# Layer norms taken by halves of 272 tokens, their variance by four groups of 32 PSUM rows, and the retention heads unrolled

## The chip, the core and the metric

The kernel runs on one core of a Trainium2 chip. The metric is the device time of one execution in microseconds; three executions of the kernel before gave 1895.0, 1896.52 and 1900.74 us, median 1896.52 us. The profiled execution is one of its own, with its own time.

## The reference, cut to what matters

Two decoder layers over 512 prompt tokens and 32 sample tokens, 544 in all, of width 1024. Layer 0 mixes by a chunk gMLP and stick-breaking attention, layer 1 by a retention with four heads. Each mixer and each feed-forward part ends in a residual addition and a layer norm over the 1024 features, so there are four layer norms:

```python
def _layer_norm(x, g, b):
    mu = jnp.mean(xf, axis=-1, keepdims=True)
    var = jnp.mean(jnp.square(xf - mu), axis=-1, keepdims=True)
    y = (xf - mu) * lax.rsqrt(var + LN_EPS)
    return y * g + b
# layer 0:  x <- LN(ALPHA*x + W_out_ab [gMLP | attention])     norm 0
# layer 1:  x <- LN(ALPHA*x + W_out_ret (silu(g) * HeadNorm(Retention)))   norm 2
# every l:  x <- LN(ALPHA*x + W_down(gelu(conv3(x W_gate)) * x W_val))     norms 1 and 3
```

The outputs are y for all tokens, new keys, values and states, and the convolution states.

## The kernel before, in words

Activations lie with features on the 128 partitions and the 544 tokens along the row: y[:, m, :] is feature block m of 8 (KD = 8). A product of weights and activations goes by output tiles of 128 features. Each weight tile is loaded by a DMA into w_raw, split by ScalarE (w_hi) and VectorE (w_lo, the function low), and multiplied in three terms (w_hi x_hi, w_hi x_lo, w_lo x_hi) for each block kt of 128 input features; x_hi and x_lo are the same split of the activations. Tokens go in two halves of 272 columns (HN), each half into a PSUM bank of its own, so a tile takes k times 3 times 2 matmuls, k being 8 after a norm or the attention, 11 (KF) in the down product and 4 in the retention's output product. All of them stand in part_body (L1267). Tiles alternate between two slots j = 0, 1: banks 0 and 1 for j = 0, banks 2 and 3 for j = 1, and one w_raw, w_hi and w_lo buffer for each j. A weight tile u can be split once tile u - 2 is done (tile_done), and TensorE starts tile u when w_lo is there (lo_ready) and its banks are free (evicted[j]).

The order on each engine is written out by hand, in program order, with semaphores between engines; nothing is scheduled. Around a norm it is this. VectorE adds each finished output tile to y and to the running sum s1 (add_up, L986 and L990). After the last tile TensorE sums s1 over the partitions (the mean, L1527, banks 4 and 5), VectorE subtracts it from the 8 blocks (L1009), ScalarE squares them (L589) into two slots of sq, and TensorE adds the squares of each block up over the partitions (L1532, banks 6 and 7). ScalarE takes Ln and Exp (L592, L594), VectorE sharpens the result by one Newton step (L1019, L1021, L1024) and scales the blocks (L1013), ScalarE shifts them into x_hi (L599; into y at the end, L602), and VectorE makes x_lo (L1034). TensorE's next product waits for x_lo block by block (ln_done). Meanwhile GpSimd prepares the residual for the next addition (L417) once all 8 blocks of x_lo stand, and the first two weight tiles of the next product have been split before the norm begins. The third one is split when the first tile of the next product is done.

After norm 1 VectorE also waits for GpSimd's scaling of y and for a zeroed tile before it goes on. The four retention heads are one loop on every engine. At the end y is stored by 8 DMAs, one for each block.

## Time and profile before

| what | us |
|---|---|
| median of three executions | 1896.52 |
| profiled execution, its own time | 1897.47 |
| its span | 1895.7 |
| TensorE busy in the span | 1778.9 |
| VectorE busy | 893.0 |
| ScalarE busy | 529.2 |
| mean granted clock of TensorE | 0.974 |

The time of the profiled execution is 1.8 us longer than its span and 1.0 us above the median. Matmuls overlap, so a busy time of TensorE close to the span says only that it seldom stood still. A row of a timeline gives the start, the time to the end of its last instruction, the engine and line, what is written and read, the count, and in brackets how long the engine had been idle and what it had waited for. A granted clock of 1.00 is TensorE's level of 2.4 GHz, 0.50 that of 1.2 GHz.

### The profile page before, as it was taken

To read this page: it belongs to the slowest core of one execution; us is meant where nothing else is said; L and a number is where in the kernel's file an instruction comes from. 1 tells how busy PE (TensorE), PEld (TensorE's weight loads), DVE (VectorE), ACT (ScalarE), POOL (GpSimd) and SP (SyncE) were. 2 spreads that over 40 slices of the span, in tenths; PEclk is the share of its full clock that TensorE was granted. 3 is DMA by queue.
4 is the path that set the end of the run, shared out by engine and by line. 5 is a ranking of instruction groups with operands and counts; after the bars stand their busy time and mean duration, and the time that the engine had idled before them with its cause. 6 is when DMAs were issued, how large, how long until landed. Compare 5 with 4: busy or idle time off the path is not lost.

```text
span 1895.7 us, 35052 instructions
## 1 busy us (share of the span) xinstructions
PE 1778.9 (94%) x13474; PEld 1591.3 (84%) x13474; DVE 893.0 (47%) x1435; ACT 529.2 (28%) x742; POOL 151.3 (8%) x137
## 2 busy tenths in 40 slices
PE   8998996979999999979989989989987999999996
PEld 8765674869999999969679759849947999999995
DVE  3444355566542555352362263263256655245543
ACT  3324233242221222142222222222223322122213
POOL 0000002001000000014003013013010100000000
PEclk9999998899999999999989999999998999999998
DMA  8889784112222223212242333333323223222221
GB/s 285 297 297 302 234 306 161 45 45 89 88 99 79 78 89 105 80 38 94 104 156 97 118 133 100 129 127 105 140 89 100 71 89 106 82 78 89 89 93 47
DMA packets 84221, 234.65 MB, mean 124 GB/s; under 512 B 9777, under 2 KB 10066, under 8 KB 83778
## 3 DMA queue, kind: packets, MB, share of 16 engines
q1 hardware_dynamic: 80834, 218.97, 34.0%
q0 software_dynamic: 3328, 14.92, 2.2%
q8 instruction: 34, 0.56, 0.1%
q14 instruction: 25, 0.20, 0.0%
HBM read 210.05 MB, written 23.80 MB: 123 GB/s over the span
## 4 chain that ended last, share of the span: by engine, by line
PE 66%; issue 25%; DVE 5%; ACT 2%; POOL 1%; DMA 1%; SPq 0%; DVEq 0%; ACTq 0%; POOLq 0%
PE banks L1267 50%; PE banks L1612 2%; PE banks L1619 2%; PE banks L1604 1%; PE banks L1532 1%; PE banks L1294 1%; PE banks L1369 1%; PE banks L1382 1%; PE banks L1592 1%; PE banks L1330 1%; POOL y L417 1%; PE banks L1358 1%; PE banks L1635 1%; DVE x_lo L1034 1%; PE banks L1372 1%
## 5 line engine op out<-in xcount | busy, mean ns | idle before, releaser
L1267 PE MATMUL banks<-x_hi,w_hi 128*128 128x272 f32 x2624 | 551.7, 292 | 33.4 <-DVE x_lo L1034 22.3
L1267 PE MATMUL banks<-x_hi,w_lo 128*128 128x272 f32 x2624 | 545.8, 290 | 0.0
L1267 PE MATMUL banks<-x_lo,w_hi 128*128 128x272 f32 x2624 | 544.9, 289 | 0.0
L694 DVE TENSOR_TENSOR w_lo<-w_raw,w_hi 128x1024 fp32r<-128x1024 f32 (+2 forms) x228 | 284.9, 1250 | 514.6 <-ACT w_hi L462 514.5
L462 ACT ACTIVATE w_hi<-w_raw 128x1024 fp32r<-128x1024 f32 (+2 forms) x228 | 238.2, 1045 | 942.3 <-PE banks L1267 913.2
L1267 PEld LDWEIGHTS banks<-x_hi,w_hi 128*128 128x128 f32 x2624 | 415.0, 190 | 51.8 <-issue 32.5
L1267 PEld LDWEIGHTS banks<-x_lo,w_hi 128*128 128x128 f32 x2624 | 416.0, 190 | 0.0
L1267 PEld LDWEIGHTS banks<-x_hi,w_lo 128*128 128x128 f32 x2624 | 413.6, 190 | 0.0
L1267 PE MATMUL banks<-act_lo,w_hi 128*128 128x272 f32 x704 | 145.3, 287 | 0.0
L1267 PE MATMUL banks<-act_hi,w_hi 128*128 128x272 f32 x704 | 145.1, 287 | 0.0
L1267 PE MATMUL banks<-act_hi,w_lo 128*128 128x272 f32 x704 | 145.1, 287 | 0.0
L986 DVE TENSOR_TENSOR y<-y,banks 128x544 f32 (+1 forms) x40 | 28.9, 721 | 188.6 <-PE banks L1267 188.6
L1267 PEld LDWEIGHTS banks<-act_hi,w_lo 128*128 128x128 f32 x704 | 110.3, 188 | 0.0
L1267 PEld LDWEIGHTS banks<-act_lo,w_hi 128*128 128x128 f32 x704 | 110.3, 188 | 0.0
L1267 PEld LDWEIGHTS banks<-act_hi,w_hi 128*128 128x128 f32 x704 | 110.2, 188 | 0.0
L1267 PE MATMUL banks<-m_hi,w_hi 128*128 128x272 f32 x256 | 57.7, 309 | 8.7 <-DVE m_lo L1197 8.7
L436 POOL TENSOR_TENSOR onat<-rqk,rope 128x544 f32<-128x544 f32 x32 | 46.6, 1486 | 154.4 <-ACT rqk L643 154.4
L1267 PE MATMUL banks<-m_lo,w_hi 128*128 128x272 f32 x256 | 56.2, 303 | 0.0
L1267 PE MATMUL banks<-m_hi,w_lo 128*128 128x272 f32 x256 | 56.1, 302 | 0.0
L449 POOL TENSOR_SCALAR km<-kp,cst 96x256 fp32r<-96x256 f32 x32 | 29.7, 932 | 302.5 <-DVE kp L1119 173.9
L1267 PEld LDWEIGHTS banks<-m_hi,w_hi 128*128 128x128 f32 x256 | 44.0, 206 | 9.2 <-issue 9.2
L1144 DVE SCALAR_TENSOR_TENSOR s<-s,tab,banks 128x1024 f32<-128x1024 f32 x32 | 40.5, 1277 | 16.0 <-PE banks L1635 15.9
(232 smaller groups left out, 1714.3 us busy)
## 6 DMA issues: line engine op xcount, KB each, us to landing
w_raw<-in_w_up SPq DMA_DIRECT2D x88, 512.0 KB, 3.2
kv<-in_kc SPq DMA_DIRECT2D x128, 256.0 KB, 4.8
kv<-in_vc SPq DMA_DIRECT2D x128, 256.0 KB, 4.4
w_raw<-in_w_rin SPq DMA_DIRECT2D x48, 512.0 KB, 3.3
w_raw<-in_w_dn SPq DMA_DIRECT2D x32, 704.0 KB, 4.1
s<-in_s SPq DMA_DIRECT2D x32, 512.0 KB, 7.3
out_ret_s<-s SPq DMA_DIRECT2D x32, 512.0 KB, 2.6
w_raw<-in_w_in_ab POOLq DMA_DIRECT2D x16, 512.0 KB, 6.1
```

Of the source, the lines that this page charges most:

```text
L417: nc.gpsimd.tensor_scalar(y[:, m, :], y[:, m, :], lnp[:, n, 1, m:m + 1], ALPHA, ALU.add, ALU.mult)\
L436: step.add(nc.gpsimd.tensor_tensor(t[n], a, rope[:, c, :], ALU.mult))
L449: nc.gpsimd.tensor_scalar(km[:, b % 2, :], kp[:, :].bitcast(F32), blockm[:, b:b + 1], None, ALU.mult).then_inc(km_ready, 1)
L462: return nc.scalar.activation(out, in_, ACT.Copy)
L694: V.tensor_tensor(w_lo[:, j, 0:k * P], w_raw[:, j, 0:k * P], w_hi[:, j, 0:k * P].bitcast(F32), ALU.subtract).then_inc(lo_ready, 1)
L986: V.tensor_tensor(out, out, bank_pair(j), ALU.add).then_inc(evicted[j], 1)
L1034: V.scalar_tensor_tensor(x_lo[:, m, :], y[:, m, :], lnp[:, n, 1, m:m + 1], x_hi[:, m, :].bitcast(F32), ALU.add, ALU.subtract)\
L1144: V.scalar_tensor_tensor(old, old, tab[:, T_CD:T_CD + 1], banks, ALU.mult, ALU.add)\
L1267: last = mm(B[:, 2 * j + half, 0:HN], a[:, j, w], x[:, kt, half * HN:(half + 1) * HN], start=kt == 0 and n == 0, stop=kt == k - 1 and n == 2)
L1294: last = mm(B[32 * r:32 * r + 32, 4, k * P:(k + 1) * P], qz[:, c, :], kv[:, s, g, c * P:(c + 1) * P], start=c == 0, stop=c == 3)
L1612: last = mm(B[:, bank, :], scT[:, c0:c0 + P], rvn[:, j, :], start=j == 0, stop=j == t)
L1619: last = mm(B[rows, 3, :], qm[:, dt, b, :], s0[:, b % RING, dt, :], start=False, stop=b >= DEC_B - 4 and dt == 1)
```

## The change

A norm is taken for tokens 0 to 271 (half 0) and 272 to 543 (half 1) apart, and its work is put between the products before and behind it.

- TensorE: the last two tiles of the product before a norm (last_pair) run half 0 of both tiles first and half 1 of both after it. Between the steps of half 1, at places that a table names, stand half 0's mean, the two parts of its variance and the sum of its parts (spread). The first two tiles of the product behind the norm (first_pair) run half 0 first, with half 1's mean, variance and spread between its steps, and then half 1. The mean takes two matmuls (s1 and y's block 7) in place of one.
- The variance: four squares lie in sq at a time, and each is multiplied into 32 rows of its own of the PSUM bank. ScalarE copies the bank to s1, divided by 32, and a matmul with ones adds the rows up.
- VectorE: half 0 and half 1 in a written order. The evictions of the last two tiles, and the w_lo splits of the next product's first two tiles, stand inside the norm. ScalarE likewise, with the w_hi splits.
- The norms' instructions on VectorE and ScalarE held 128 x 544 elements; each is now two of 128 x 272.
- The heads are unrolled on all engines. VectorE's wait for the zeroed tile stands after the first head's products, and its wait for GpSimd's scaling of y ahead of the output addition.
- GpSimd waits for x_lo of both halves. y is stored by 16 DMAs, half 0 first.

The diff, cut; the removed lines of norm on each engine stand in the kernel above.

```diff
...
+PLACES = {KF: ((0, 3), (0, 10), (1, 4), (1, 7)), KD: ((0, 3), (1, 1), (1, 6), (1, 7)), 4: ((0, 3), (1, 3), (1, 3), (1, 3))}
...
+        def sq_slot(m):
+            return sq[:, m % 4 // 2, cols(m % 2)]
...
+            for half in range(2):
+                for m in range(KD):
+                    sp.wait_ge(y_final, half * KD + m + 1)
+                    sp.dma_start(A["yT"][:, m, cols(half)], y[:, m, cols(half)]).then_inc(y_stored, 16)
...
+            def norm(n, u):
                 nc.scalar.preload_act_table_set("natural_log_exp_and_others")
...
+                def squares(half, first, end):
+                    for m in range(first, end):
+                        q = half * KD + m
+                        act.wait_ge(c_ready, 2 * n * KD + q + 1)
+                        if q >= 4:
+                            act.wait_ge(sq_used, 4 * n + q // 4)
+                        nc.scalar.activation(sq_slot(m), y[:, m, cols(half)], ACT.Square).then_inc(sq_ready, 1)
+                def parts(half):
+                    act.wait_ge(sq_used, 4 * n + 2 * half + 2)
+                    nc.scalar.activation(s1[:, cols(half)], B[:, 6 + half, 0:HN], ACT.Copy, scale=1.0 / 32)\
+                        .then_inc(part_ready, 1)
+                def deviation(half):
+                    act.wait_ge(var_done, 2 * n + half + 1)
+                    step.add(nc.scalar.activation(std[:, cols(half)], B[:, 6 + half, 0:HN], ACT.Ln, bias=eps))
+                    step.wait()
+                    nc.scalar.activation(std[:, cols(half)], std[:, cols(half)], ACT.Exp, scale=-0.5)\
+                        .then_inc(std_ready, 1)
+                def shift(half, first, end):
+                    for m in range(first, end):
+                        act.wait_ge(scaled, (2 * n + half) * KD + m + 1)
+                        dst, done = (x_hi, lnhi_ready) if n < 3 else (y, y_final)
+                        nc.scalar.activation(dst[:, m, cols(half)], y[:, m, cols(half)], ACT.Identity,
+                                             bias=lnp[:, n, 1, m:m + 1]).then_inc(done, 1)
+                squares(0, 0, 4)
+                if u is not None:
+                    split(u, 0, KD)
+                squares(0, 4, KD)
+                parts(0)
+                deviation(0)
+                shift(0, 0, 3)
+                if u is not None:
+                    split(u + 1, 1, KD)
+                for m in range(3, KD):
+                    shift(0, m, m + 1)
+                    squares(1, 2 * m - 6, min(2 * m - 4, KD))
+                parts(1)
+                deviation(1)
+                shift(1, 0, KD)
...
+            def norm(n, base, u):
+                def take(half, j):
+                    i = N_OUT - 2 + j
+                    if half == 0:
+                        dve.wait_ge(half_done, 2 * n + j + 1)
+                    else:
+                        dve.wait_ge(tile_done, base + i + 1)
+                    last = V.tensor_tensor(y[:, i, cols(half)], y[:, i, cols(half)], B[:, 2 * j + half, 0:HN], ALU.add)
+                    if half:
+                        last.then_inc(evicted[j], 1)
+                    elif j:
+                        last.then_inc(s_sum, 1)
+                    else:
+                        step.add(last)
+                    if j == 0:
+                        if half:
+                            dve.wait_ge(evicted[0], (base + N_OUT) // 2 + 1)
+                        else:
+                            step.wait()
+                        step.add(V.tensor_tensor(s1[:, cols(half)], s1[:, cols(half)], y[:, i, cols(half)], ALU.add))
+                def centre(half):
+                    dve.wait_ge(m_done, 2 * n + half + 1)
+                    for m in range(KD):
+                        V.tensor_tensor(y[:, m, cols(half)], y[:, m, cols(half)], B[:, 4 + half, 0:HN], ALU.subtract)\
+                            .then_inc(c_ready, 1)
+                def inverse(half):
+                    own, first, var = s1[:, cols(half)], std[:, cols(half)], B[:, 6 + half, 0:HN]
+                    dve.wait_ge(std_ready, 2 * n + half + 1)
+                    step.add(V.tensor_tensor(own, first, first, ALU.mult))
+                    step.wait()
+                    step.add(V.scalar_tensor_tensor(own, var, eps, own, ALU.add, ALU.mult))
+                    step.wait()
+                    step.add(V.scalar_tensor_tensor(first, own, 3.0, first, ALU.subtract, ALU.mult))
+                    step.wait()
+                    dve.wait_ge(c_ready, (2 * n + half + 1) * KD)
+                def scale(half, m):
+                    V.scalar_tensor_tensor(y[:, m, cols(half)], y[:, m, cols(half)], lnp[:, n, 0, m:m + 1],
+                                           std[:, cols(half)], ALU.mult, ALU.mult).then_inc(scaled, 1)
+                def rest(half, m):
+                    if n < 3:
+                        dve.wait_ge(scaled, (2 * n + half) * KD + m + 1)
+                        dve.wait_ge(lnhi_ready, (2 * n + half) * KD + m + 1)
+                        V.scalar_tensor_tensor(x_lo[:, m, cols(half)], y[:, m, cols(half)], lnp[:, n, 1, m:m + 1],
+                                               x_hi[:, m, cols(half)].bitcast(F32), ALU.add, ALU.subtract)\
+                            .then_inc(ln_done[half], 1)
+                def tail(half, first):
+                    for m in range(first, KD):
+                        scale(half, m)
+                        rest(half, m - 1)
+                    rest(half, KD - 1)
                 step.wait()
...
+                take(0, 0)
                 step.wait()
...
+                take(0, 1)
+                dve.wait_ge(s_sum, 2 * n + 1)
+                centre(0)
+                take(1, 0)
                 step.wait()
...
+                if u is not None:
+                    low(u, 0, KD)
+                inverse(0)
+                scale(0, 0)
+                scale(0, 1)
+                take(1, 1)
+                dve.wait_ge(evicted[1], (base + N_OUT) // 2 + 1)
+                dve.sem_inc(s_sum, 1)
+                rest(0, 0)
+                scale(0, 2)
+                rest(0, 1)
+                scale(0, 3)
+                rest(0, 2)
+                centre(1)
+                scale(0, 4)
+                rest(0, 3)
+                if u is not None:
+                    low(u + 1, 1, KD)
+                scale(0, 5)
+                rest(0, 4)
+                tail(0, 6)
+                inverse(1)
+                scale(1, 0)
+                tail(1, 1)
...
-            dve.wait_ge(y_scaled, 1 + 2 * KD)
-            dve.wait_ge(zeroed, 3)
...
+                dve.wait_ge(zeroed, 3)
...
+                dve.wait_ge(y_scaled, 1 + 2 * KD)
...
+            def half_step(j, half, k, hi, lo, kt):
+                w = slice(kt * P, (kt + 1) * P)
+                for n, (a, x) in enumerate(((w_hi, hi), (w_hi, lo), (w_lo, hi))):
+                    last = mm(B[:, 2 * j + half, 0:HN], a[:, j, w], x[:, kt, cols(half)],
+                              start=kt == 0 and n == 0, stop=kt == k - 1 and n == 2)
+                return last
+            def mean(n, half):
+                if half:
+                    pe.wait_ge(s_sum, 2 * n + 2)
+                else:
+                    pe.wait_ge(s_sum, 2 * n + 1)
+                mm(B[:, 4 + half, 0:HN], mean_mat, s1[:, cols(half)], start=True, stop=False)
+                mm(B[:, 4 + half, 0:HN], mean_mat, y[:, KD - 1, cols(half)], start=False, stop=True).then_inc(m_done, 1)
+            def variance(n, half, m0):
+                pe.wait_ge(sq_ready, (2 * n + half) * KD + m0 + 4)
+                for g in range(4):
+                    last = mm(B[32 * g:32 * g + 32, 6 + half, 0:HN], mean_mat[:, 0:32], sq_slot(m0 + g),
+                              start=m0 == 0, stop=m0 == 4)
+                last.then_inc(sq_used, 1)
+            def spread(n, half):
+                pe.wait_ge(part_ready, 2 * n + half + 1)
+                mm(B[:, 6 + half, 0:HN], ones, s1[:, cols(half)], start=True, stop=True).then_inc(var_done, 1)
+            def last_pair(n, base, k, hi, lo):
+                for half in range(2):
+                    for j in range(2):
+                        u = base + N_OUT - 2 + j
+                        if half == 0:
+                            pe.wait_ge(lo_ready, u + 1)
+                            pe.wait_ge(evicted[j], u // 2 + 1)
+                        for kt in range(k):
+                            last = half_step(j, half, k, hi, lo, kt)
+                            if half:
+                                for at, what in zip(PLACES[k], ((mean, ()), (variance, (0,)), (variance, (4,)), (spread, ()))):
+                                    if at == (j, kt):
+                                        what[0](n, 0, *what[1])
+                        last.then_inc(half_done if half == 0 else tile_done, 1)
+            def first_pair(n, base):
+                def step_of(half, j, kt):
+                    if j == 0:
+                        pe.wait_ge(ln_done[half], n * KD + kt + 1)
+                    elif kt == 0:
+                        pe.wait_ge(lo_ready, base + 2)
+                        pe.wait_ge(evicted[1], base // 2 + 1)
+                    last = half_step(j, half, KD, x_hi, x_lo, kt)
+                    if half and kt == KD - 1:
+                        last.then_inc(tile_done, 1)
+                pe.wait_ge(lo_ready, base + 1)
+                pe.wait_ge(evicted[0], base // 2 + 1)
+                step_of(0, 0, 0)
+                mean(n, 1)
+                step_of(0, 0, 1)
+                step_of(0, 0, 2)
+                variance(n, 1, 0)
+                step_of(0, 0, 3)
+                step_of(0, 0, 4)
+                variance(n, 1, 4)
+                step_of(0, 1, 0)
+                step_of(0, 1, 1)
+                step_of(0, 0, 5)
+                spread(n, 1)
+                for kt in range(2, 6):
+                    step_of(0, 1, kt)
+                for kt in range(6, KD):
+                    step_of(0, 0, kt)
+                for kt in range(6, KD):
+                    step_of(0, 1, kt)
+                for kt in range(KD):
+                    step_of(1, 0, kt)
+                    if kt >= 2:
+                        step_of(1, 1, kt - 2)
+                for kt in range(KD - 2, KD):
+                    step_of(1, 1, kt)
...
-            product(U_OUT_AB, N_OUT, KD, x_hi, x_lo, mixed)
-            norm(0)
+            product(U_OUT_AB, N_OUT - 2, KD, x_hi, x_lo, mixed)
+            last_pair(0, U_OUT_AB, KD, x_hi, x_lo)
             ffn(0)
-            norm(1)
-            with pe.Fori(0, H_C) as h:
-                with pe.Fori(0, N_RIN // 2) as i:
+            last_pair(1, U_RET - N_OUT, KF, act_hi, act_lo)
...
```

In the rows below, s is s1, cst holds the constant matrices (the mean's and ones) and banks is PSUM. The first place is VectorE from the last tile of the product before norm 0 on. Before:

```order
L986 TENSOR_TENSOR y<-y,banks 128x544
L990 TENSOR_TENSOR s<-s,y 128x544
L694 TENSOR_TENSOR w_lo<-w_raw,w_hi 128x1024
L1009 TENSOR_TENSOR y<-y,banks 128x544 x8
L1019 TENSOR_TENSOR s<-std 128x544
L1021 SCALAR_TENSOR_TENSOR s<-banks,cst,s 128x544
L1024 SCALAR_TENSOR_TENSOR std<-s,std 128x544
L1013 SCALAR_TENSOR_TENSOR y<-y,lnp,std 128x544 x2
L1034 SCALAR_TENSOR_TENSOR x_lo<-y,lnp,x_hi 128x544
```

And the changed kernel on VectorE, from half 0's mean (L1070) to half 1's (the second L1070):

```order
L1070 TENSOR_TENSOR y<-y,banks 128x272 x8
L1053 TENSOR_TENSOR y<-y,banks 128x272
L1065 TENSOR_TENSOR s<-s,y 128x272
L735 TENSOR_TENSOR w_lo<-w_raw,w_hi 128x1024
L1076 TENSOR_TENSOR s<-std 128x272
L1078 SCALAR_TENSOR_TENSOR s<-banks,cst,s 128x272
L1080 SCALAR_TENSOR_TENSOR std<-s,std 128x272
L1085 SCALAR_TENSOR_TENSOR y<-y,lnp,std 128x272 x2
L1053 TENSOR_TENSOR y<-y,banks 128x272
L1092 SCALAR_TENSOR_TENSOR x_lo<-y,lnp,x_hi 128x272
...
L1070 TENSOR_TENSOR y<-y,banks 128x272 x8
```

The eviction of the last tile's half 1 (the second L1053) now stands ahead of the first x_lo, and half 1's subtraction follows after three blocks of half 0's x_lo.

The second place is TensorE between the product before norm 0 and the one behind it. Before, the norm stands between the two:

```order
L1267 MATMUL banks<-x_hi,w_lo 128x272 x2
L1250 REGISTER_ALU
L1250 COMPARE_AND_BRANCH
L1527 MATMUL banks<-s,cst 128x272 x2
L1532 MATMUL banks<-sq,cst 128x272 x16
L1250 UNCONDITIONAL_BRANCH
```

In the changed kernel, from the last step of last_pair to half 1's first variance (L1376 is the spread, L1364 and L1365 the mean, L1370 the variance):

```order
L1376 MATMUL banks<-s,cst 128x272
L1355 MATMUL banks<-x_hi,w_hi 128x272
L1355 MATMUL banks<-x_lo,w_hi 128x272
L1355 MATMUL banks<-x_hi,w_lo 128x272
L1364 MATMUL banks<-s,cst 128x272
L1365 MATMUL banks<-y,cst 128x272
...
L1355 MATMUL banks<-x_hi,w_lo 128x272
L1370 MATMUL banks<-sq,cst 32x272 x4
```

One step of the next product stands between half 0's spread and half 1's mean, and two more before the variance; the sixteen wide matmuls of the variance are now four times four narrow ones.

## Rows read from the trace of the kernel before

**Rows 1.** Timeline of TensorE at norm 0: start us, us, engine and line.
```profile
396.44 0.41 PE L1267 MATMUL banks<-x_hi,w_lo 128*128 128x272 f32 x2
398.49 1.18 PE L1527 MATMUL banks<-s,cst 128*128 128x272 f32 x4 [1.64 <-DVE s L990]
401.17 6.08 PE L1532 MATMUL banks<-sq,cst 128*128 128x272 f32 x24 [1.50 <-ACT sq L589]
...
415.94 0.79 PE L1267 MATMUL banks<-x_hi,w_hi 128*128 128x272 f32 x2 [6.42 <-DVE x_lo L1034]
...
425.17 0.52 PE L1267 MATMUL banks<-x_hi,w_hi 128*128 128x272 f32 x2
```
**Rows 2.** Windows: us, busy PE, PEld, DVE, ACT, POOL, granted clock, DMA share, GB/s.
```profile
426.00:808.00 382.00, 382.00 (x3056) 382.00 (x3055) 188.92 (x321) 92.92 (x146) 6.47 (x7) 1.00 0.26 88
```
**Rows 3.** Timeline of VectorE at norm 0.
```profile
399.71 5.14 DVE L1009 TENSOR_TENSOR y<-y,banks 128x544 f32<-128x544 f32 x8
411.00 0.73 DVE L1019 TENSOR_TENSOR s<-std 128x544 f32<-128x544 f32 x1 [6.15 <-ACT std L594]
...
415.01 0.79 DVE L1034 SCALAR_TENSOR_TENSOR x_lo<-y,lnp,x_hi 128x544 fp32r<-128x544 f32 x1 [0.19 <-ACT x_hi L599]
415.71 0.78 DVE L1013 SCALAR_TENSOR_TENSOR y<-y,lnp,std 128x544 f32<-128x544 f32 x1
...
427.32 1.79 DVE L694 TENSOR_TENSOR w_lo<-w_raw,w_hi 128x1024 fp32r<-128x1024 f32 x1 [2.19 <-ACT w_hi L462]
```
**Rows 4.** Timeline of ScalarE at norm 0.
```profile
400.46 1.29 ACT L589 ACTIVATE sq<-y 128x544 f32<-128x544 f32 x2 [1.16 <-DVE y L1009]
...
426.23 1.06 ACT L462 ACTIVATE w_hi<-w_raw 128x1024 fp32r<-128x1024 f32 x1 [0.70 <-PE banks L1267]
```
**Rows 5.** Timeline of VectorE in layer 0's feed-forward part.
```profile
434.52 0.43 DVE L1066 TENSOR_TENSOR af<-ge,banks 128x272 f32<-128x272 f32 x1
434.87 0.40 DVE L1067 TENSOR_TENSOR af<-ge,banks 128x240 f32<-128x240 f32 x1
```
**Rows 6.** Groups of ScalarE's instructions: count, busy us, mean ns, idle before.
```profile
L462 ACT ACTIVATE gp<-banks 128x272 f32<-128x272 f32 x132 | 32.1, 316 | 0.0
L599 ACT ACTIVATE x_hi<-y,lnp 128x544 fp32r<-128x544 f32 x24 | 17.8, 749 | 22.0 <-DVE y L1013 22.0
```
**Rows 7.** Timeline of TensorE in the attention, four products of 32 rows each.
```profile
241.27 1.10 PE L1330 MATMUL banks<-kv,ad 128*32 128x512 f32 x8 [0.35 <-DMA kv<-in_vc]
```
**Rows 8.** Windows of TensorE alone at norms 0 and 3: us, busy, clock.
```profile
413.00:420.00 7.00, 4.06 (x18) 0.51 0.00 0
1870.60:1877.40 6.80, 5.30 (x13) 0.50 0.00 0
```
**Rows 9.** Timeline of TensorE at norm 1.
```profile
816.12 0.41 PE L1267 MATMUL banks<-act_hi,w_lo 128*128 128x272 f32 x2
...
853.33 0.49 PE L1267 MATMUL banks<-x_hi,w_hi 128*128 128x272 f32 x2 [1.71 <-DVE w_lo L694]
```
**Rows 10.** Timeline of VectorE behind norm 1.
```profile
851.64 0.07 DVE L1097 MEMSET rmv<- 128x10 f32 x1 [7.12 <-POOL qm L426]
```
**Rows 11.** Timeline of TensorE at norm 2.
```profile
1447.54 0.41 PE L1267 MATMUL banks<-m_hi,w_lo 128*128 128x272 f32 x2
...
1466.82 0.79 PE L1267 MATMUL banks<-x_hi,w_hi 128*128 128x272 f32 x2 [6.42 <-DVE x_lo L1034]
```
**Rows 12.** Timeline of VectorE ahead of norm 2's last tile.
```profile
1443.40 0.69 DVE L694 TENSOR_TENSOR w_lo<-w_raw,w_hi 128x512 fp32r<-128x512 f32 x1
```
**Rows 13.** Timelines of TensorE and ScalarE at norm 3.
```profile
1867.29 0.41 PE L1267 MATMUL banks<-act_hi,w_lo 128*128 128x272 f32 x2
...
1872.54 10.31 PE L1532 MATMUL banks<-sq,cst 128*128 128x272 f32 x32 [1.50 <-ACT sq L589]
...
1887.49 5.62 ACT L602 ACTIVATE y<-y,lnp 128x544 f32<-128x544 f32 x8 [3.19 <-DVE y L1013]
```
**Rows 14.** The chain that ended last, across the end of a head (start us, us).
```profile
966.88 99.39 PE banks L1267 x768
```

More of the change, by code:

```diff
@@ L339, in _ @@
             load_ffn(0)
-            with sp.Fori(0, H_C) as h:
+            for h in range(H_C):
                 base = h * N_RET + U_RET
@@ L427, in _ @@
             pool.wait_ge(rope_in, 16)
-            with pool.Fori(0, H_C) as h, step.loop(h, H_C, 8):
+            for h in range(H_C):
                 for qk in range(2):
@@ L1678, in _ @@
                         tile_body(j, 4, m_hi, m_lo)
-            norm(2)
+            last_pair(2, U_FFN[1] - N_OUT, 4, m_hi, m_lo)
             ffn(1)
-            norm(3)
-RET_STEPS = 14 + 9
+            last_pair(3, U_ALL - N_OUT, KF, act_hi, act_lo)
+            mean(3, 1)
+            for m in (0, 4):
+                variance(3, 1, m)
+            spread(3, 1)
 def decays(h):
```

174 lines of the change are left out of this document (64 added, 110 removed).

## The prediction

> **What bounds the kernel now.** I read the windows over the products first. In layer 0's feed-forward part TensorE is busy for 382 of 382 us at the full clock, with 3056 matmuls, one each 0.125 us [rows 2]. There nothing can be won but by fewer matmuls, and the change leaves their number. Then I read TensorE's timeline at the norms. The last matmul of the product before norm 0 starts at 396.44, the next product's first at 415.94, and its last step only at 425.17 [rows 1]: 48 matmuls that need 6.0 us take 10. So I take as one stretch the time from the start of the last pair of tiles to the start of the third tile behind the norm; everything that the change moves lies in it.
>
> Before, the stretches are these, with 0.125 us for a matmul. Norm 0: the pair has 96 matmuls, so it starts at 396.69 - 12.0 = 384.7; the third tile starts at 425.17 + 0.75 + 6.0 = 431.9; 47.2 us. Norm 1: 132 matmuls, 816.37 - 16.5 = 799.9, to 853.33 [rows 9]; 53.5. Norm 2: 48 matmuls, 1447.8 - 6.0 = 1441.8; its product starts at 1466.82 [rows 11] and runs as norm 0's, 16.0 more to 1482.8; 41.0. Norm 3: 1867.54 - 16.5 = 1851.0, to the last shift's end at 1893.1 [rows 13]; 42.1, with the last store behind it in both kernels.
>
> VectorE's and ScalarE's timelines show what fills a gap: subtraction (5.14), squares behind it, Ln and Exp, three Newton operations, then scaling and x_lo in turn, 1.4 us a block [rows 3, 4]. TensorE waits 6.42 us for the first x_lo and after it goes at VectorE's pace [rows 1, 3].
>
> **The costs of a half.** A 272-column operation of VectorE that takes two tensors lasts 0.43 and lets the next start after 0.35 [rows 5]; I take 0.36. The scaling kind lasts 0.79 at 544 columns and starts every 0.70 [rows 3]; 272 columns less are 0.28 less, so 0.50 and 0.41. Two dependent ones cost the first's whole duration. ScalarE: a square 1.29 / 2 less 0.28, so 0.36, Ln and Exp 0.4 each, copy 0.32, shift 0.75 less 0.28, so 0.47 [rows 4, 6]. A fp32 mean matmul is 1.18 / 2, less the tail, so 0.50 [rows 1]. A handover between engines is 0.05 to 0.2 with the matmul's own tail.
>
> Four 32-row products: in the attention four of 512 columns took 1.10 us together [rows 7], so they ran side by side: one of 512 columns alone takes about 0.5 x 512 / 272 = 0.94. For 272 columns that is 0.6. The variance falls from 16 x 0.5 = 8.1 us (6.08 for three quarters [rows 1]) to 4 x 0.6. Added are two mean matmuls and two spreads, 2.0, and two copies of 0.3. TensorE's own work in a norm goes from 9.3 to about 5.4.
>
> **Norm 0, step by step**, from the pair's start. Half 0 of both tiles ends at 6.0. VectorE adds the last tile by 6.8. The mean stands four steps (0.375 each) into half 1, 7.6 to 8.6. VectorE subtracts 8.75 to 11.6, the eighth square ends at 13.0 (a weight split of 1.0 lies between), the second variance part 13.3 to 13.9, the copy, the spread to 14.9. That hides this half's norm behind half 1's matmuls but for its end: Ln and Exp to 16.0, three Newton operations to 17.6, two scalings, the last eviction, x_lo to 19.4. TensorE starts at 19.5, idle 4.5. Half 1's mean ends at 20.9. VectorE, after three blocks of x_lo, subtracts from 21.0 to 23.9, then scales block 4. Only behind that may ScalarE shift block 4 and make squares 3 and 4 (25.6): TensorE, which stands in order at the variance, waits 4.0. The next one waits for squares 7 and 8: 28.7, another 1.5. Spread to 30.9, Ln, Exp, Newton, two scalings and x_lo to 35.2; TensorE has had ten steps of half 0 to do meanwhile and idles 1.3. Then VectorE gives a block every 0.83 and TensorE two steps in 0.75, to 41.0, and three steps are left: 42.4.
>
> Then a wait that was not there. The third tile's weights can be split once tile 1 is done. Before, the second tile (6.0 us) covered that. Now the two tiles end 1.1 apart. The split takes 1.06 [rows 4]; w_lo takes 1.79 beside GpSimd's residual work, which again starts at this moment [rows 3]. With handovers that is 3.2 less 1.1: 2.1 of idle TensorE. Queued behind w_lo on VectorE is the first convolution, for which nothing waits for 6 us. Norm 0: 44.5 against 47.2, -2.7 at the full clock.
>
> **The other norms**, by the same steps. Norm 1's pair is longer by 36 matmuls, so the first half's chain ends under it but for x_lo, which now waits for the last eviction: idle 3.4. I get 45.8 + 2.1 = 47.9 against 53.5: -5.6. In it is the old wait of 1.71 for w_lo, caused by VectorE's wait for the zeroed tile [rows 9, 10]; that goes, and the 2.1 come in its place. Norm 2's pair has 48 matmuls, half 1 of it 3.0 us, which cover little: its last tile starts after 1.5 but its w_lo is there after 2.3 [rows 12], 0.8 lost, the variance parts wait 0.7 and 1.8, the spread 0.6. 40.0 + 2.1 against 41.0: +1.1. Norm 3: half 1's mean at 22.2, variance 28.0 and 30.6, shifts end 38.8 against 42.1: -3.3. The sum at the full clock is -10.5.
>
> **The clock.** Before, TensorE's clock was 0.51 from 413 to 420, after the 6.4 us of idleness, and 0.50 from 1870.6 to 1877.4 [rows 8], where it had only waited twice for 1.5 to 2 us with a mean between. So the level of 1.2 GHz comes after sparse stretches, not only after empty ones, and lasts some 7 us. Before, it cost little in norms 0 to 2, since x_lo set the pace. Now half 1's mean, variance and spread stand in the chain. With 1.2 GHz from 19 to 31 or so, the mean costs 1.0 more, the steps in front of it 0.3, variance and spread 0.5 each: 2.3 in norm 0, 1.7 in norm 1, 2.3 in norm 2 (its spread and two variances), 1.4 in norm 3. The ends are 0 and 3.2 each, the latter with the clock low from 16 to 34. Taken: 2.3 + 1.7 + 2.3 + 1.4 = 7.7. The norms then stand at -0.4, -3.9, +3.4 and -1.9: -2.8.
>
> The Trainium skill, "TensorE: Matmul & The Clock Gate", section "HAM oscillation — how this bites in real kernels", tells of a loop whose waits throttle the clock again at every turn. By it the bursts and waits of each first pair would pay more than once; that is the second rival below. No row here shows such a pattern at a norm.
>
> **Heads unrolled.** The chain runs from 966.88 for 99.39 us through 768 matmuls and over a head's end [rows 14]; at 0.125 these need 96.0 and the rest is slow ones at the stretch's start, so the loop's turn costs TensorE nothing. What may go is register work ahead of waits; what may come is longer code to fetch. Neither has a row. I bound it by -3 and +4 for all heads and take -1. VectorE's later wait for y's scaling, 16 DMAs for 8 at the end, and the GpSimd waits: nothing, each is ready long before; the last store starts with the last shift as before.
>
> **The sum.** -2.8 - 1 = -3.8. The profiled execution took 1897.47, 1.0 above the median; against the median of 1896.5 I predict 1892.7.
>
> **The rivals.** First, the chains are tighter or the clock stays up: the times between the halves are then those of the full-clock sum, -10.5 - 1, 1885. For it speaks that norm 0 before kept 1.00 through two waits of 1.5 and 1.6 (the clock fell only later); against it the 0.50 at norm 3. Also for it: the places in last_pair may fit better than my sums of small handovers. Second, slower: the clock stays at 1.2 GHz through half 1 of each first pair. It decides there, because two steps then take 1.36 us where VectorE gives a block every 0.83; 16 steps cost 10.9 for 6.6. Norm 0 would take 52.0, norm 1 55.3, norm 2 49.6, norm 3 40.6: +4.8, +1.8, +8.6, -1.5, in all +13.7, so 1909. Against it: each slow stretch before ended within 7 us under dense matmuls. It decides from the point where the clock has not risen 14 us after the first x_lo. Third, the four groups run one after another: 16 parts at 0.5 instead of 4 at 0.6 put 5.5 on each norm's chain, +22 on -10.5, 1908; rows 7 speak against it, and it is also the case in which the change doesn't do what it says. Fourth, VectorE's small operations pay their fixed part in full: 0.43 and 0.50 instead of the spacings 0.36 and 0.41 make the norms' chains 2.4, 2.3, 2.5 and 1.4 longer, +8.6 on the forecast, 1901; rows 5 speak against it.
>
> The rule behind the fourth is in the Trainium skill, "VectorE: DVE Perf Modes", section "The TRN2 errata — SBUF-src ops pay a fixed extra latency per instruction", which advises tiles of 512 elements and more; 272 lies below. The measured spacing of 0.35 at 272 columns bears a small fixed part, not the full one.
>
> **The numbers.** Forecast 0.50, first 0.34, second 0.05, third 0.04, fourth 0.07. What can be told from no change is 0.3%, 5.7 us. The forecast at -3.8, with 4 to either side, has 0.10 of its 0.50 below -5.7 and 0.02 above +5.7. Faster: 0.32 of the first and 0.10, 0.42. Slower: 0.02 + 0.05 + 0.04 + 0.03 = 0.14. Same 0.44. The range from 1884 to 1900 takes in the full-clock sum and the forecast with all clock terms at their upper end.
>
> **What would show it.** Right: the first matmul behind norm 0 some 19.5 us after its pair's start; waits of 4 and 1.5 us at the second half's two variances; a wait near 2 us for w_lo ahead of each third tile; the stretches at 44.5 to 47, 48 to 50, 42 to 45 and 39 to 41 us; norm 2 not gaining. Wrong: a variance part over 1 us at full clock, VectorE's spacing above 0.45, a granted clock of 0.50 in half 1 of the first pair, or heads that differ from those before by more than 1 us each.

## The result and the profile after

The changed kernel takes 1907.18 us, the median of four runs (1906.24 to 1910.88), against 1895.99 us for the kernel before in the same series (four runs, 1895.0 to 1900.74): 1.0058 times as long, with a 95% interval of 1.0036 to 1.0079. It is slower by some 11 us; predicted was 1892.7 with a range of 1884 to 1900. The profiled execution took 1906.24 us, 8.8 us more than the one before; its span is 1904.1 us, 8.4 more. The mean granted clock fell from 0.974 to 0.966.

I cut the time at the same places as the prediction: from the start of the last pair of tiles ahead of a norm to the start of the third tile behind it.

| stretch, us | before | predicted, full clock | predicted, forecast | measured |
|---|---|---|---|---|
| norm 0 (383.49 to 432.81) | 47.2 | 44.5 | 46.8 | 49.3 |
| norm 1 (801.02 to 856.02) | 53.5 | 47.9 | 49.6 | 55.0 |
| norm 2 (1443.73 to 1491.00) | 41.0 | 42.1 | 44.4 | 47.3 |
| norm 3 (1860.73 to the last shift's end) | 42.1 | 38.8 | 40.2 | 40.6 |

The measured stretches are 2.1, 1.5 and 6.3 us longer than before and 1.5 shorter, +8.4, which is the whole difference of the spans. (Counted matmul by matmul in the trace of before, norms 0 and 2 took 47.4 and 41.2 us there; then the stretches give +8.1 and the rest +0.3.) What lies between the stretches comes out even, but not piece by piece. The clock falls once more at the third tile of norm 1, and at that of norm 2, just behind the end of the stretch. After (first two rows) and before at the same tile of norm 1 (last row), in windows as explained below:

```profile
856.00:861.00 5.00, 4.98 (x22) 4.98 (x23) 2.19 (x1) 0.00 (x0) 5.00 (x4) 0.50 0.70 200
1492.50:1496.00 3.50, 3.50 (x18) 3.50 (x17) 3.22 (x5) 0.67 (x1) 1.11 (x2) 0.51 0.48 189
```

```profile
853.40:858.40 5.00, 5.00 (x40) 5.00 (x41) 0.78 (x1) 0.00 (x0) 4.97 (x4) 1.00 0.66 207
```

The first 24 matmuls of norm 1's third tile take 5.4 us where they took 3.1, and from norm 2's third tile to norm 3's pair it is 369.7 us for 368.1. Against that, the part from norm 1's third tile to norm 2's pair, where the heads are, took 587.7 us and not 588.4, slow start included, and the first pair starts 1.2 us earlier. So in sum the loss is at the norms and right behind them.

Norm 0 first. TensorE's timeline after, with the start, the length, the engine and line, what is written and read, and in brackets the idle time and what ended it (compare [rows 1]):

```profile
383.49 0.29 PE L1355 MATMUL banks<-x_hi,w_hi 128*128 128x272 f32 x1
...
403.70 0.57 PE L1355 MATMUL banks<-x_hi,w_hi 128*128 128x272 f32 x1 [4.65 <-DVE x_lo L1092]
...
404.51 1.11 PE L1364 MATMUL banks<-s,cst 128*128 128x272 f32 x2
...
411.10 1.14 PE L1370 MATMUL banks<-sq,cst 128*32 128x272 f32 x8 [3.52 <-ACT sq L611]
...
422.28 0.39 PE L1355 MATMUL banks<-x_hi,w_hi 128*128 128x272 f32 x1 [1.20 <-DVE x_lo L1092]
...
432.81 0.52 PE L1443 MATMUL banks<-x_hi,w_hi 128*128 128x272 f32 x2 [1.83 <-DVE w_lo L735]
```

The waits stand where the prediction put them: 4.65 us for the first x_lo (predicted 4.5) 20.2 us after the pair's start (19.5), 3.52 at half 1's variance (4.0), 1.20 at half 1's first x_lo (1.3), 1.83 for the third tile's w_lo (2.1). One is missing: at half 1's second variance 0.32 us were left of 1.5, since the slow steps ahead of it fill the time (at the full clock of experiment 1, added work and wait take 1.4 us there). What else is not as predicted is the length of what stands between them. The windows of the same stretch (us, busy time of PE, PEld, DVE, ACT and POOL with counts, granted clock, DMA share, GB/s) say why:

```profile
404.00:408.00 4.00, 3.59 (x13) 2.90 (x12) 2.63 (x8) 2.65 (x5) 0.00 (x0) 0.61 0.00 0
408.00:411.00 3.00, 0.00 (x0) 0.00 (x0) 3.00 (x8) 1.11 (x3) 0.00 (x0) 0.92 0.00 0
411.00:414.00 3.00, 2.80 (x14) 1.61 (x14) 2.84 (x7) 2.20 (x7) 0.00 (x0) 0.50 0.41 115
...
421.00:424.00 3.00, 1.42 (x8) 0.92 (x7) 2.75 (x8) 1.96 (x4) 0.00 (x0) 1.00 0.00 0
424.00:428.00 4.00, 4.00 (x20) 4.00 (x21) 3.69 (x10) 2.77 (x6) 0.00 (x0) 0.57 0.02 6
428.00:431.00 3.00, 2.98 (x24) 2.76 (x23) 0.02 (x1) 1.73 (x3) 2.89 (x5) 1.00 0.00 0
```

TensorE's clock falls to 1.2 GHz three times, from 403.7 to 407.1, 410.5 to 417.3 and 424.2 to 427.6: after the wait for the first x_lo, after the wait for the squares, and after the wait for half 1's first x_lo. In between it comes back to 2.4 GHz. Before, it fell once in this norm, ahead of steps that were waiting for VectorE anyway [rows 8]. Now the mean, the variance and the spread of half 1 stand in what falls (1.11 us for two mean products, 1.14 for a variance part), and the last steps of half 1 do too.

Norm 1 has something of its own. VectorE and GpSimd behind it, in their timelines:

```profile
851.14 4.75 DVE L735 TENSOR_TENSOR w_lo<-w_raw,w_hi 128x1024 fp32r<-128x1024 f32 x1 [3.07 <-ACT w_hi L475]
```

```profile
849.24 5.57 POOL L429 TENSOR_SCALAR y<-y,lnp 128x544 f32<-128x544 f32 x8
854.76 0.51 POOL L439 MEMSET qm<- 128x512 f32 x1
```

```profile
856.02 0.82 PE L1443 MATMUL banks<-x_hi,w_hi 128*128 128x272 f32 x2 [4.94 <-DVE w_lo L735]
```

The w_lo split, 1.79 us beside the same work of GpSimd before [rows 3], takes 4.75 here and ends 1.1 us after GpSimd's scaling of y (855.89 and 854.81). Alone it takes 1.23, so VectorE got next to nothing done on it while GpSimd ran. TensorE waits 4.94 us for it, which gives back the wait of 1.71 that went [rows 9] and more. Behind norm 1 of the kernel before, the two did not meet:

```profile
845.45 5.60 POOL L417 TENSOR_SCALAR y<-y,lnp 128x544 f32<-128x544 f32 x8
851.82 2.36 DVE L694 TENSOR_TENSOR w_lo<-w_raw,w_hi 128x1024 fp32r<-128x1024 f32 x2
```

VectorE's wait for the zeroed tile [rows 10], which the change took away as a cost, had kept it back until GpSimd was done. Behind norms 0 and 2 the same instruction took 1.69 and 1.67, and TensorE waited 1.83 and 1.81.

### The profile page after: what moved, and what is told of

Its sections match the earlier page's. It is cut to its first block, busy times and chain, and to the rows that moved or that the text cites. A ratio compares the mean times of both kernels' runs of the same rounds, so it can differ in the third digit from the quotient of the medians.

```text
span 1904.1 us, 34366 instructions
## 1 busy us (share of the span) xinstructions
PE 1778.3 (93%) x13506; PEld 1586.2 (83%) x13506; DVE 906.7 (48%) x1543; ACT 541.9 (28%) x822; POOL 149.8 (8%) x137
## 4 chain that ended last, share of the span: by engine, by line
PE 86%; DVE 7%; ACT 3%; issue 2%; DMA 1%; SPq 0%; ACTq 0%; DVEq 0%
PE banks L1443 67%; PE banks L1355 4%; PE banks L1779 2%; PE banks L1786 2%; PE banks L1771 1%; PE banks L1545 1%; PE banks L1470 1%; PE banks L1759 1%; PE banks L1558 1%; DMA kv<-in_vc 1%; PE banks L1506 1%; PE banks L1548 1%; DVE y L1070 1%; PE banks L1802 1%; DVE w_lo L735 1%
## 5 line engine op out<-in xcount | busy, mean ns | idle before, releaser
L1443 PE MATMUL banks<-x_hi,w_hi 128*128 128x272 f32 x2496 | 522.7, 291 | 18.1 <-DVE w_lo L735 8.6
L1443 PE MATMUL banks<-x_hi,w_lo 128*128 128x272 f32 x2496 | 518.4, 289 | 0.0
L1443 PE MATMUL banks<-x_lo,w_hi 128*128 128x272 f32 x2496 | 517.3, 289 | 0.0
L1443 PEld LDWEIGHTS banks<-x_hi,w_hi 128*128 128x128 f32 x2496 | 394.6, 190 | 32.7 <-issue 20.1
L1443 PEld LDWEIGHTS banks<-x_lo,w_hi 128*128 128x128 f32 x2496 | 395.2, 190 | 0.0
L1443 PEld LDWEIGHTS banks<-x_hi,w_lo 128*128 128x128 f32 x2496 | 392.0, 190 | 0.0
L1443 PE MATMUL banks<-act_lo,w_hi 128*128 128x272 f32 x616 | 127.0, 287 | 0.0
L1443 PE MATMUL banks<-act_hi,w_hi 128*128 128x272 f32 x616 | 126.9, 287 | 0.0
L1443 PE MATMUL banks<-act_hi,w_lo 128*128 128x272 f32 x616 | 126.8, 287 | 0.0
L1443 PEld LDWEIGHTS banks<-act_lo,w_hi 128*128 128x128 f32 x616 | 96.5, 188 | 0.0
L1443 PEld LDWEIGHTS banks<-act_hi,w_lo 128*128 128x128 f32 x616 | 96.5, 188 | 0.0
L1355 PE MATMUL banks<-x_hi,w_hi 128*128 128x272 f32 x128 | 46.6, 364 | 17.5 <-DVE x_lo L1092 17.5
L449 POOL TENSOR_TENSOR onat<-rqk,rope 128x544 f32<-128x544 f32 x32 | 47.3, 1506 | 154.8 <-ACT rqk L684 154.8
L1443 PE MATMUL banks<-m_hi,w_lo 128*128 128x272 f32 x240 | 52.4, 301 | 0.0
L1355 PEld LDWEIGHTS banks<-x_hi,w_hi 128*128 128x128 f32 x128 | 29.0, 226 | 27.5 <-issue 20.2
```

The costliest lines, as they stand in the source:

```text
L449: step.add(nc.gpsimd.tensor_tensor(t[n], a, rope[:, c, :], ALU.mult))
L1355: last = mm(B[:, 2 * j + half, 0:HN], a[:, j, w], x[:, kt, cols(half)], start=kt == 0 and n == 0, stop=kt == k - 1 and n == 2)
L1443: last = mm(B[:, 2 * j + half, 0:HN], a[:, j, w], x[:, kt, half * HN:(half + 1) * HN], start=kt == 0 and n == 0, stop=kt == k - 1 and n == 2)
```

## The experiments

My theory was then: the instruction schedule is as worked out, and the loss is the clock (about 10 us, three falls where I had charged one) and VectorE beside GpSimd (about 3 us, behind norm 1). The rivals: waits and handovers longer than worked out at any clock, and heads that got slower. Eight kernels ran in two series of four. Kernels of one series share the runs of the kernel before, whose median was 1898.89 us in the first (23 runs) and 1898.38 in the second (29 runs).

**1. Keep the clock up.** Matmuls that nobody reads are put into TensorE's waits, sized so that they end before the data come.

```diff
+            def keep_busy(bank, times):
+                for _ in range(times):
+                    mm(B[:, bank, 0:HN], w_hi[:, 0, 0:P], w_hi[:, 0, 0:HN], start=True, stop=True)
...
                 pe.wait_ge(evicted[0], base // 2 + 1)
+                keep_busy(5, (30, 22, 30)[n])
                 step_of(0, 0, 0)
...
+                keep_busy(4, 26)
                 variance(n, 1, 0)
...
+                keep_busy(4, 8)
                 variance(n, 1, 4)
...
+                keep_busy(4, 8)
                 for kt in range(KD):
                     step_of(1, 0, kt)
```

In norm 3 there are 18 ahead of half 1's mean, and 30 and 12 ahead of its variance parts.

> The changed kernel with extra matmuls of weights with weights, whose result nobody reads, in TensorE's waits: 30, 22 and 30 (3.75, 2.75, 3.75 us) ahead of the first x_lo behind norms 0, 1 and 2, 26 and 8 ahead of half 1's two variance parts, 8 ahead of half 1's first step, and 18, 30 and 12 ahead of norm 3's mean and variance parts. Theory clock: the clock that falls three times in each first pair is what the forecast missed; with it up, the stretches of norms 0, 1, 2 go from 49.3, 55.0 and 47.3 us to about 45, 51 and 43.5, norm 3 gives 1.5, in all 12 to 14 us, to about 1894. Theory VectorE: the chain is set by VectorE's and ScalarE's operations and by handovers; then less than 3 us go, and the time stays above 1904.

Measured: 1893.40 us (5 runs, 1889.54 to 1897.98), ratio to the kernel before 0.9962 [0.9948, 0.9976]. The same places of norm 0:

```profile
411.04 3.42 PE L1380 MATMUL banks<-w_hi 128*128 128x272 f32 x26
415.02 0.67 PE L1370 MATMUL banks<-sq,cst 128*32 128x272 f32 x8 [0.57 <-ACT sq L611]
...
424.73 0.39 PE L1355 MATMUL banks<-x_hi,w_hi 128*128 128x272 f32 x1 [0.23 <-DVE x_lo L1092]
...
433.89 0.51 PE L1451 MATMUL banks<-x_hi,w_hi 128*128 128x272 f32 x2 [1.70 <-DVE w_lo L735]
```

The pair starts at 388.79 here. TensorE still waits 0.57 us for the squares after the added work, so that work delays nothing; it only keeps the level. The variance part takes 0.67 us and not 1.14. Counted from the pair's start, the first x_lo comes at 20.1 (20.2 in the changed kernel), the first variance part at 26.2 (27.6), half 1's first step at 35.9 (38.8) and the third tile at 45.1 (49.3). So the first fall cost 1.4 us, the second 1.5 and the third 1.4, 4.2 before rounding. The stretches are 45.1, 52.4 and 43.2 us, against 49.3, 55.0 and 47.3. The clock theory holds, and its term is worth 14 us, 1907.2 less 1893.4. The changed kernel has no run in this series; by the ratios to the kernel before, 0.9962 here and 1.0058 and 1.0039 in the two series that have it, it would be 15 to 18. In norm 1 the wait for w_lo is not cured: it is 6.16 us, with 0.50 behind it, and w_lo takes 5.96.

**2. Move GpSimd away.** In the changed kernel, GpSimd scales y one tile later.

```diff
             def scale_residual(n):
                 for half in range(2):
                     pool.wait_ge(ln_done[half], n * KD + KD)
+                pool.wait_ge(lo_ready, (U_FFN[0] + 3, U_RET + 4, U_FFN[1] + 3)[n])
```

> The changed kernel, but GpSimd begins to scale y behind norms 0, 1 and 2 only when the w_lo of the third tile (for norm 1 of the third and fourth) is made. Theory GpSimd: its scaling starves VectorE's w_lo behind norm 1 (4.75 us instead of 1.22); w_lo takes 1.22 in all three places, the waits of TensorE ahead of the third tile go from 1.8, 4.9 and 1.8 to 1.4 each, 4.5 us in all, to about 1902.5. Rival: the 4.75 us come from the transfers that land at that moment or from the split; then the wait stays above 4 us and the time does not move by more than 1.

Measured: 1899.69 us (12 runs, 1896.08 to 1906.02), ratio 1.0006 [0.9995, 1.0016].

```profile
854.04 1.23 DVE L736 TENSOR_TENSOR w_lo<-w_raw,w_hi 128x1024 fp32r<-128x1024 f32 x1 [3.10 <-ACT w_hi L476]
```

```profile
855.40 0.51 PE L1444 MATMUL banks<-x_hi,w_hi 128*128 128x272 f32 x2 [1.42 <-DVE w_lo L736]
...
869.49 0.51 PE L1444 MATMUL banks<-x_hi,w_hi 128*128 128x272 f32 x2 [1.81 <-DVE w_lo L736]
```

Nothing on VectorE changed but what GpSimd does beside it, and w_lo takes 1.23 us for 4.75. The wait ahead of norm 1's third tile is 1.42, and a new one of 1.81 comes a tile later, where GpSimd now rotates the rope product; the w_lo made there takes 6.48 us, so the meeting of the two engines has moved and is not gone. The stretches are 48.8, 51.7 and 45.7. The fall at norm 1's third tile is gone with the wait, and one stands behind the new wait instead (0.50 over 871 to 874.4). The gain of the median, 7.5 us against the changed kernel of the other series, is more than the 4.5 expected, and the profiled execution, the slowest of the twelve (1906.02), shows no gain in total: it lost 3.2 us before norm 0 and 2.6 from norm 1's third tile to norm 2. What the difference beyond the waits is stays open.

**3. Both.** Experiments 1 and 2 in one kernel.

> Both edits together. If the two causes are apart the gains add up: 16 to 18 us, to about 1890, 6 us below the kernel before. If the low clock was what let VectorE fall together with GpSimd's work, less than the sum goes.

Measured: 1889.28 us (6 runs, 1881.93 to 1892.54), ratio 0.9942 [0.9925, 0.996]. This beats both kernels. In this series it is 4.1 us faster than experiment 1 and 10.4 faster than experiment 2, so the fill is worth 10.4 us where GpSimd is out of the way.

```profile
404.00:408.00 4.00, 3.20 (x23) 2.88 (x22) 3.77 (x11) 2.92 (x6) 0.00 (x0) 1.00 0.00 0
411.00:414.00 3.00, 2.84 (x22) 2.02 (x22) 2.94 (x7) 2.20 (x8) 0.00 (x0) 1.00 0.43 119
424.00:428.00 4.00, 4.00 (x33) 3.93 (x31) 2.21 (x7) 3.34 (x5) 0.00 (x0) 1.00 0.00 0
```

The stretches are 44.8, 47.7 and 42.6 us, and 39.1 to the last shift's end in norm 3 (1844.73 to 1883.87). The prediction's sums at the full clock were 44.5, 47.9, 42.1 and 38.8. So the first rival of this list, longer handovers, is refuted to about a microsecond a norm: the sums hold 2.1 us of wait for w_lo beside GpSimd, and without GpSimd that wait is 1.36, 1.43 and 1.37 here, so that the rest of the chain is 0.5 to 1.3 longer than worked out.

**4. Heads alone.** The kernel before with its loop over the heads written out on all five engines (`for h in range(H_C)` for each `Fori`), and nothing else.

> The kernel before with its four heads unrolled on all engines and nothing else. Theory: unrolling moves the time by -1 to 0 us, since the stretch from the third tile behind norm 1 to the last pair before norm 2 went from 588.5 to 587.7 us. Rival: longer code costs several us outside the norms, hidden there by something else; then this one is slower by over 3 us.

Measured: 1897.30 us (11 runs, 1894.41 to 1901.73), ratio 0.9995 [0.9986, 1.0004]. The heads are neither the loss nor a gain that can be told from none.

**5. The changed kernel again**, in the second series.

> The changed kernel as it is, in one series with the kernel before and the three below, so that all are compared on one chip. Expected: 11 us (0.6%) over the kernel before, and the same three falls of the granted clock in each of norms 0, 1 and 2.

Measured: 1907.00 us (6 runs, 1905.58 to 1911.75), ratio 1.0039 [1.0026, 1.0052]. That is 8.6 us over the kernel before, where 11 were expected. Its stretches are 49.3, 53.7 and 47.3 us: norms 0 and 2 repeat, with the same falls. Norm 1 does not; there the clock was low once, for 10 us (0.53 over 832 to 843), and at 1.00 from 843 to 857, where the first profile has three falls. Behind norm 1 w_lo took 5.95 us beside GpSimd:

```profile
855.82 5.95 DVE L735 TENSOR_TENSOR w_lo<-w_raw,w_hi 128x1024 fp32r<-128x1024 f32 x1 [1.87 <-ACT w_hi L475]
```

**6. Fill in the kernel before.** Is the fill a gain that any kernel would have?

```diff
+                if n == 3:
+                    keep_busy(12)
                 for m in range(KD):
                     pe.wait_ge(sq_ready, n * KD + m + 1)
...
+                if n < 3:
+                    pe.wait_ge(lo_ready, (U_FFN[0], U_RET, U_FFN[1])[n] + 1)
+                    keep_busy(46)
```

> The kernel before, with matmuls that nobody reads in TensorE's long wait for the first x_lo of norms 0, 1 and 2 (46 of 128x272, 0.113 us each at 2.4 GHz = 5.2 of 6.4 us), and 12 between the means and the first square of norm 3. It asks whether what fill gives is a gain of the changed kernel alone. Clock theory: the kernel before loses its clock once in a norm, at 1.2 GHz for 4 us of steps after the wait (at 0.51 of full over 416 to 420), so fill gives 2 us in each of three norms and some 5 us in norm 3, whose 32 matmuls took 10.31 us at 0.50: together 8 to 10 us, time about 1888 against 1898. Rival: VectorE's splits are the bound at the start of the next product, and each TensorE step there waits 0.37 us for them; then a faster TensorE only waits longer, and the fill gives 1 to 3 us in the three norms together.

Measured: 1896.59 us (12 runs, 1894.44 to 1900.47), ratio 0.9991 [0.998, 1.0002]: 1.8 us less, and the interval reaches none. My expectation of 8 to 10 was wrong and its rival right in norms 0 to 2.

```profile
411.56 6.12 PE L1526 MATMUL banks<-w_hi 128*128 128x272 f32 x46
418.36 0.49 PE L1267 MATMUL banks<-x_hi,w_hi 128*128 128x272 f32 x2 [0.67 <-DVE x_lo L1034]
...
419.66 0.52 PE L1267 MATMUL banks<-x_hi,w_hi 128*128 128x272 f32 x2 [0.31 <-DVE x_lo L1034]
```

```profile
412.00:416.00 4.00, 4.00 (x34) 4.00 (x33) 2.49 (x4) 1.34 (x2) 0.00 (x0) 1.00 0.02 4
416.00:420.00 4.00, 3.02 (x22) 2.61 (x21) 3.81 (x6) 2.20 (x3) 0.00 (x0) 1.00 0.00 0
```

The clock is held at 1.00 over 416 to 420, where it was 0.51, and TensorE turns all of it into waits of 0.31 to 0.38 us for VectorE's x_lo at each step. A slow clock that stands under another engine's pace costs nothing: from the product's first step to the third tile it is 16.10, 17.98 and 16.10 us in norms 0, 1 and 2, and 16.09, 17.98 and 16.11 before. Norm 3 did gain there: its 32 variance matmuls took 7.97 us for 10.31 [rows 13], and its stretch 41.0 for 42.1.

The profile shows something else that the median hides. The clock fell in the variance of norms 0 and 1, ahead of the fill, where the kernel before had kept 1.00:

```profile
402.00:406.00 4.00, 3.96 (x10) 3.04 (x11) 3.72 (x6) 1.50 (x3) 0.00 (x0) 0.57 0.25 97
```

The 24 variance matmuls of norm 0 took 7.63 us for 6.08 [rows 1], and the stretches of norms 0 and 1 are 48.9 and 56.0 us for 47.4 and 53.5. The code and the waits there (1.64 and 1.50 us) are those of before. So the same waits cost a fall in one execution and none in another.

**7 and 8. The fill of experiment 1 in two parts**: only the one ahead of half 0's first x_lo, and only the others.

> The changed kernel with fill only ahead of the first x_lo of half 0 (30, 22 and 30 matmuls in norms 0, 1 and 2), none in the later waits. Theory that each fall is a matter of the wait just before it: only the first fall of a pair goes (0.61 over 404 to 408 in norm 0); the waits of 3.5 us for the squares and of 1.2 us for half 1's first x_lo keep their own falls; gain 1.2 to 1.6 us in each of three norms, 4 to 5 us in all. Rival, that the later falls follow from the first: all three go, and the gain comes near the 14 us of full fill.

> The changed kernel with fill in the later waits alone (ahead of half 1's variance parts, of its first x_lo, and in norm 3), none ahead of the first x_lo of half 0. Theory that each fall is a matter of the wait just before it: the first fall stays, the second and third go, and norm 3 runs at full clock: gain 8 to 10 us of the 14. Rival, that the later falls follow from the first: they stay in spite of the fill, and the gain is norm 3's, 1 to 2 us.

Measured: the first part alone 1903.78 us (12 runs, 1897.61 to 1908.05), ratio 1.0024 [1.0013, 1.0036], 3.2 less than the changed kernel in this series. The rest alone 1899.40 us (12 runs, 1895.63 to 1903.04), ratio 1.0001 [0.9992, 1.001], 7.6 less; expected were gains of 4 to 5 and of 8 to 10. With the first part alone, the windows of norm 0 (first three rows), norm 1 (the fourth) and norm 2:

```profile
408.00:411.00 3.00, 2.24 (x14) 1.48 (x14) 2.94 (x7) 2.20 (x7) 0.00 (x0) 0.68 0.34 79
411.00:414.00 3.00, 2.64 (x15) 1.78 (x16) 0.77 (x2) 1.11 (x3) 0.00 (x0) 0.50 0.24 96
424.00:428.00 4.00, 3.45 (x27) 3.17 (x25) 1.93 (x6) 3.63 (x8) 2.20 (x4) 1.00 0.00 0
837.00:845.00 8.00, 7.21 (x41) 6.77 (x42) 5.84 (x15) 4.59 (x8) 1.31 (x3) 0.79 0.03 3
1466.00:1469.00 3.00, 2.79 (x15) 1.93 (x16) 0.62 (x2) 0.96 (x3) 0.00 (x0) 0.50 0.19 75
1477.00:1486.00 9.00, 7.34 (x56) 7.02 (x56) 6.47 (x15) 5.86 (x10) 5.37 (x7) 1.00 0.10 19
```

The second fall stays in all three norms, as the theory of separate falls says. The third stays in norm 1 and is gone in norms 0 and 2, which had no fill ahead of it: there the rival has a point. The profiled execution was the fastest of the twelve; their spread of 10 us may come from this fall being there or not, which one profile can't show. With the rest alone, the waits behind the fill are 0.37, 0.19 and 0.21 us in norm 0, and the second and third falls are gone. The parts add up to 10.8 us, against some 13.6 for all of the fill in the other series. In norm 1 the fall at the third tile stays in both, behind the wait for w_lo, which takes 4.71 and 5.94 us there.

## Why the prediction was wrong

- **The schedule: right.** The full-clock sums are met within 0.5 us in each stretch once the clock is held and GpSimd is moved (experiment 3); part of that is luck, since the w_lo wait is 0.7 shorter than in the sums and the chain ahead of it that much longer. VectorE's spacing at 272 columns came out at 0.41 for the scaling kind, as taken. Four 32-row products side by side, at 2.4 GHz, take 0.67 us for a group of eight records, 0.6 taken. The third rival is refuted by it, the fourth by the spacing.
- **The clock: this step failed.** The prediction took "1.2 GHz from 19 to 31 or so" as one spell at 2.3, 1.7 and 2.3 us and gave half 1 back the full clock. In the profiled execution there were three falls in each of norms 0 to 2, worth 1.4, 1.5 and 1.4 us in norm 0: 4.2 for 2.3. The time at 1.2 GHz was nearly as set down, 13.6 us for 12; what was wrong is where it lies. The first two falls lie within 19 to 34 us after the pair's start and cost 2.9 for 2.3. The third, 41 to 44 us after it, in the half that had been given back the full clock, cost 1.4 for nothing. Outside the stretches, a fall at the third tile of norms 1 and 2 had no term at all. Over all norms full fill gains some 14 us (10.4 with GpSimd moved) where 7.7 had been set down. The upper end, 3.2 a norm, was too low as well, since it still knew one spell only. I knew from norm 3 before that two short waits of 1.5 to 2 us can be followed by a fall [rows 13, 8], though nearly the same two left 1.00 in norm 0, and the schedule that I had worked out has such waits ahead of half 1's variance and again at its first x_lo; I did not price that risk at each of my own waits. Whether a given wait costs a fall was not the same in each execution (experiments 5, 6 and 7). The prediction's own sign of being wrong, 0.50 in half 1 of a first pair, came (0.57 over 424 to 428, 0.50 over 425 to 427). The clock returned under dense work after some 3 to 6 us, where 7 were taken, and each of the later falls comes after such a return.
- **Which falls count.** That a slow clock cost little before was right for the reason given: held at 1.00 behind norms 0 to 2, the steps up to the third tile take as long as before (experiment 6). The change put mean, variance and spread, and steps closer to VectorE's pace, into those spells.
- **The second rival** (1909) has the right size and most of the pattern of stretches, +4.8, +1.8, +8.6 and -1.5 against +2.1, +1.5, +6.3 and -1.5, but not the mechanism: the clock did not stay down through half 1, it fell again. What was held against it was not quite so either: the kernel before has a slow stretch of 10 us in the heads (0.50 over 962.7 to 972.7, TensorE busy for 7.7 of them), and so has norm 2 of the changed kernel (0.50 over 1455 to 1465). The rule of the Trainium skill that stands there, "TensorE: Matmul & The Clock Gate", section "HAM oscillation — how this bites in real kernels", that waits within a sequence throttle the clock once more at each turn, is in kind what the windows show, 0.61, 0.50 and 0.57 with 1.00 between; that not every wait costs a fall, experiment 7 shows. The rival had a chance of 0.05.
- **GpSimd: mis-sized.** The 1.79 us for w_lo held in norms 0 and 2 (1.69, 1.67). Behind norm 1 it was 4.75 and 5.95 in two executions, 3.0 and 4.2 us more than taken, and TensorE waited 4.94 and 6.15 us where 2.1 had been set down. Every kernel with the changed norms and GpSimd's work in its old place has it (4.71 to 5.96 in five profiles), and each time w_lo ends 1.1 us after GpSimd's scaling. The step that failed is "that goes, and the 2.1 come in its place": the old wait of 1.71 had stood between GpSimd's work and w_lo, and nothing took its place.
- **Norm 2** was rightly the norm that loses, 42.1 at full clock against 41.0; its 6.3 us are that and the falls. **Norm 3** gained 1.5 for 1.9. **The heads**: -1 taken. The trace has -0.7 for the part that holds them, with 2.3 us of slow start in it, so 3.0 less without; experiment 4, heads alone, has +0.1 in its profile and no difference that can be told in the median. Where the 3.0 come from stays open.

So the schedule with its clock held and GpSimd moved is 9.6 us faster than the kernel before (1889.3 against 1898.9), and 7 faster than that kernel with a fill of its own (1896.6). The clock took 10 (experiment 3 against 2) to 14 us from it, and GpSimd 4 (experiment 3 against 1) to 7.5 (experiment 2 against the changed kernel, in another series).

## What to carry to other kernels

When a chain is cut so that TensorE gets several short waits for one long one, read each wait of the new schedule, down to the last one behind the chain, as a place where its clock may fall, and price the work behind each of them at 1.2 GHz if it is on the chain. Matmuls that nobody reads, sized to end just before the data come, are a cheap remedy, but only where TensorE and not another engine sets the pace behind the wait. Where a large fp32 operation of GpSimd starts at the moment that VectorE's next critical operation does, start it later, and before a wait is taken out, see which two engines it keeps apart.

## What was not expected of the hardware

- A fall of the clock came after a wait as short as 1.20 us behind 3 us of dense work and short ones of 0.19 (from 422.28 on; 0.57 over 424 to 428). In experiment 7, waits of 1.08, 0.18 and 0.19 at the same place of norm 0 left it at 1.00.
- VectorE's subtraction of two operands of 128x1024 took 1.23 us alone, and 1.69, 4.75 and 5.95 beside the same fp32 scaling on GpSimd. Where VectorE was slowed most, GpSimd's eight scalings took 5.57 us, as long as with no w_lo beside them (5.60 before, norm 1); beside the w_lo of 1.69 they took 6.74, and beside one of 1.55 in experiment 1, 8.78. What decides which of the two is served is open.
- The time up to norm 0 differs from execution to execution though the instructions are the same: the last pair ahead of norm 0 started at 382.12, 383.49, 384.86, 386.74, 388.79, 389.25 and 389.33 us in seven profiled kernels. In the changed kernel that is most of the difference of the totals (the two profiled executions of the changed kernel differ by 5.5 us, and by 5.8 at this point). The clock accounts for much of it: up to there it was low for 21 us in the one that starts at 383.49 and for 31 in the one at 389.25 (over 70 to 90 it is 1.00 in the first and 0.83 in the second).
